# A two-block model on one core: sums over partitions as two float32r products of a high and a low part

## The reference

```python
def rms_norm(x, g):
    y = x32 * lax.rsqrt(jnp.mean(x32 * x32, axis=-1, keepdims=True) + NORM_EPS)
    return y * g

# first block, each of 2 layers: h = rms_norm(x, norm_g); proj = h @ w_in; three branches; x + merged @ w_out
q = apply_rope(rms_norm(qc.reshape(b, t, 4, 128), q_norm), cos_a, sin_a)
k = apply_rope(rms_norm(kc.reshape(b, t, 4, 128), k_norm), cos_a, sin_a)
# beside it the delta-rule branch: a triangular solve of 64x64 blocks, and a top-k of 128 keys
# second block: rmsnorm over 1024, 8 query heads and 2 x 2 key heads of 64, each rmsnormed;
# then h + merged @ w_o, rmsnorm over 1024, h + square(relu(hn @ w_ff1)) @ w_ff2
```

## Time and profile before

| | |
|---|---|
| median of 3 runs | 1946.79 us (1946.22 to 1951.45) |
| profiled execution | 1947.63 us, of which the span of instructions is 1945.8 |
| PE busy | 1931.6 us, 99% of the span |
| PEld busy | 1532.9 us |
| DVE, ACT, POOL busy | 1021.6, 888.9, 851.3 us |
| granted TensorE clock | full in all 40 slices |

### The profile page before, as it was taken

The page is one execution under the profiler, slowest core; times in us unless marked ns, Lnnn a source line. Parts: engine busy times, 40 slices in busy tenths (PEclk is TensorE's granted clock), DMA queues, the critical chain, the costliest instruction groups (busy, mean ns, idle before and its releaser), DMA issues.

```text
span 1945.8 us, 23734 instructions
## 1 busy us (share of the span) xinstructions
PE 1931.6 (99%) x9108; PEld 1532.9 (79%) x9108; DVE 1021.6 (53%) x1832; ACT 888.9 (46%) x1355; POOL 851.3 (44%) x644
## 2 busy tenths in 40 slices
PE   9999999999999999999999999999999999999999
PEld 6878877877788878787877788677766788888887
DVE  5657755555745668666464747574644436101210
ACT  6455553344345455543344355586555444312321
POOL 4545432443445454422434445455322445444443
PEclk9999999999999999999999999999999999999999
DMA  5334542423535235632424545322111332222232
GB/s 202 128 110 135 139 137 73 162 76 118 187 107 175 90 114 147 162 109 71 153 65 141 189 154 162 136 76 98 65 56 55 119 107 89 98 97 98 98 114 71
DMA packets 94864, 227.69 MB, mean 117 GB/s; under 512 B 29880, under 2 KB 32952, under 8 KB 93440
## 3 DMA queue, kind: packets, MB, share of 16 engines
q1 hardware_dynamic: 89056, 223.03, 35.4%
q10 hardware_dynamic: 5696, 3.15, 0.6%
HBM read 194.01 MB, written 24.64 MB: 112 GB/s over the span
## 4 chain that ended last, share of the span: by engine, by line
PE 85%; DVE 7%; DMA 2%; ACT 2%; POOL 1%; SPq 1%; issue 1%; ACTq 0%; DVEq 0%
PE bank L442 84%; DVE ER L376 1%; DVE kv L376 1%; PE bank L446 1%; SPq L371 1%; POOL wl L376 1%; DMA X<-inverses 1%; DMA gt<-gates 1%; DVE scs L401 1%; DMA kv<-blocks 1%; DVE m8s L398 0%; ACT lt L428 0%; DVE lt L386 0%; DVE tmp L376 0%; ACT wh L431 0%
## 5 line engine op out<-in xcount | busy, mean ns | idle before, releaser
L376 POOL TENSOR_TENSOR wl<-st,wh 128x512 fp32r<-128x512 f32 x602 | 804.5, 1359 | 1019.3 <-ACT wh L431 1019.2
L442 PE MATMUL bank<-hh,wh 128*128 128x512 f32 x1616 | 651.8, 404 | 2.8 <-DVE hl L386 0.9
L442 PE MATMUL bank<-hh,wl 128*128 128x512 f32 x1616 | 629.8, 390 | 0.0
L442 PE MATMUL bank<-hl,wh 128*128 128x512 f32 x1616 | 629.3, 390 | 0.0
L431 ACT ACTIVATE wh<-st 128x1024 fp32r<-128x1024 f32 (+1 forms) x302 | 317.0, 1050 | 242.9 <-PE bank L442 194.5
L442 PEld LDWEIGHTS bank<-hh,wh 128*128 128x128 f32 x1616 | 303.4, 188 | 92.5 <-issue 24.6
L442 PEld LDWEIGHTS bank<-hl,wh 128*128 128x128 f32 x1616 | 303.6, 188 | 66.9 <-issue 6.9
L442 PEld LDWEIGHTS bank<-hh,wl 128*128 128x128 f32 x1616 | 303.3, 188 | 64.3
L376 DVE TENSOR_TENSOR xt<-xt,bank 128x512 f32<-128x512 f32 x40 | 27.5, 687 | 235.6 <-PE bank L442 235.6
L428 ACT ACTIVATE tmp<-bank 128x512 f32<-128x512 f32 x70 | 41.7, 596 | 156.8 <-PE bank L442 150.2
L442 PE MATMUL bank<-fh,wh 128*128 128x512 f32 x256 | 99.6, 389 | 0.0
(11 more groups left out here) (344 smaller groups left out, 2838.6 us busy)
## 6 DMA issues: line engine op xcount, KB each, us to landing
st<-units SPq DMA_DIRECT2D x300, 512.0 KB, 3.5
gates<-tmp SPq DMA_DIRECT2D x48, 256.0 KB, 2.8
gt<-gates SPq DMA_DIRECT2D x48, 256.0 KB, 3.7
pads<-tmp SPq DMA_DIRECT2D x32, 128.0 KB, 2.7
qk<-tmp SPq DMA_DIRECT2D x16, 256.0 KB, 4.3
x_scratch<-xt SPq DMA_DIRECT2D x2, 2048.0 KB, 8.7
xt<-x_scratch SPq DMA_DIRECT2D x2, 2048.0 KB, 8.3
ph<-phi SPq DMA_DIRECT2D x8, 512.0 KB, 4.6
```

The costliest lines, as they stand in the source:

```text
L376: return NOTHING if self.e is None else self.e.tensor_tensor(out, a, b, op)
L442: return NOTHING if self.e is None else self.e.matmul(out, lhsT, rhs, start=start, stop=stop, skip_group_check=share)
```

## The change

The constants `onesr`, `meanr` and `blkr` become float32r tiles of their own, filled by DVE at the start out of a zeroed tile, and leave the DMA of constants (961 instead of 1345 columns); older float32 uses read them as float32. For 25 of the 26 sums of 512 columns the squares are given as two float32r parts: a high one, which ACT writes by a second Square (or by a copy of `nacc`), and a low one, which DVE gets by subtracting; PE's `summed` adds two float32r products with the same constant. `norm("in")` keeps its float32 product. In `proj(l)` all follow-up steps from the product on stand one `yield`, half a tile, later; the high and low parts have one buffer each (`sqh`, `sql`), so ACT waits for the product of row c-1 before it writes row c. In `proj2` the last query's and the last key's products stand behind the first of three units of token values.

```diff
+        def summed(out, exact, high, low):
+
+            pe.mm(out, exact, high, True, False)
+            return pe.mm(out, exact, low, False, True)
...
         def norm(w, frees):
             def total():
...
+                if w == "in":
+                    pe.wait_ge(*at("nacc", w, 7))
+                    pe.mm(bank(7, "norm", w), ones, nacc[:], True, True).then_inc(*sig("norm_mm", w))
+                else:
+                    pe.wait_ge(*at("sum_lo", w))
+                    summed(bank(7, "norm", w), onesr[:], tmpr[0][:], tmpr[1][:]).then_inc(*sig("norm_mm", w))
...
             def row(c):
                 yield
-                pe.wait_ge(*at("qk_sq", l, c))
-                pe.mm(bank(3, "qk_mean", l, c), mean, row_tiles(c)[2][:], True, True).then_inc(*sig("qk_mean", l, c))
+                yield
+                pe.wait_ge(*at("qk_lo", l, c))
+                summed(bank(3, "qk_mean", l, c), meanr[:], layer[l].sqh[:], layer[l].sql[:]).then_inc(*sig("qk_mean", l, c))
...
-                pe.wait_ge(*at("q2_sq", c))
-                pe.mm(bank(4, "q2_mm", c), blk, tmp[c % 2][:], True, True).then_inc(*sig("q2_mm", c))
+                yield
+                pe.wait_ge(*at("q2_lo", c))
+                summed(bank(4, "q2_mm", c), blkr[:], oh[:, c, :], ol[:, c, :]).then_inc(*sig("q2_mm", c))
...
+                for j in range(3):
+                    yield tokens(j), idle(1)
```

ACT, in `norm`, `row(c)` and `headnorm`:

```diff
+            if w != "in":
+                ac.wait_ge(*at("nacc", w, 7))
+                ac.cp(tmpr[0][:], nacc[:]).then_inc(*sig("sum_hi", w))
...
                 ac.act(x2[:], x[:], ACT.Square).then_inc(*sig("qk_sq", l, c))
+                if c > 0:
+                    ac.wait_ge(*at("qk_mean", l, c - 1))
+                ac.act(layer[l].sqh[:], x[:], ACT.Square).then_inc(*sig("qk_hi", l, c))
+                yield
                 yield
...
             ac.act(a[:, 0:width], x, ACT.Square, 0.125).then_inc(*sig(*sq))
+            ac.act(high, x, ACT.Square, 0.125).then_inc(*sig(*hi))
+            yield
```

DVE, in `norm`, `row(c)` and `turned`:

```diff
+            if w != "in":
+                dv.wait_ge(*at("sum_hi", w))
+                dv.tt(tmpr[1][:], nacc[:], tmpr[0][:].bitcast(F32), ALU.subtract).then_inc(*sig("sum_lo", w))
...
                 yield
+                dv.wait_ge(*at("qk_hi", l, c))
+                dv.tt(L.sql[:], x2[:], L.sqh[:].bitcast(F32), ALU.subtract).then_inc(*sig("qk_lo", l, c))
                 dv.wait_ge(*at(f"swap{c % 2}", "qk", l, c, 64))
-                dv.wait_ge(*at("qk_sq", l, c))
                 dv.stt(x[:], x[:], K(f"{w}n{l}"), TA("cosA"), ALU.mult, ALU.mult).then_inc(*sig("qk_n", l, c, 0))
                 dv.stt(xs, xs, K(f"{w}swap{l}"), TA("sinA"), ALU.mult, ALU.mult).then_inc(*sig("qk_n", l, c, 1))
+                yield
                 yield
```

More of the change, by code:

```diff
@@ L530, in build @@
     cst = sb("cst", [128, n_cst])
+    onesr, meanr, blkr = [sb(n, [128, 128], F32R) for n in ("onesr", "meanr", "blkr")]
     identr = sb("identr", [128, 128], F32R)
@@ L534, in build @@
     hh, hl = sb("hh", [128, 8, T], F32R), sb("hl", [128, 8, T], F32R)
+    tms = ExitStack()
+    tmpr = [sb(f"tmpr{i}", [128, T], F32R, stack=tms) for i in range(2)]
+    tms.close()
     tmp = [sb(f"tmp{i}", [128, T]) for i in range(4)]
@@ L594, in build @@
         L.cdiag = sb(f"cdiag{l}", [128, 128], stack=dtmp)
+        L.sqh, L.sql = [sb(f"{n}{l}", [128, T], F32R, stack=dtmp) for n in ("sqh", "sql")]
         dtmp.close()
@@ L700, in K @@
         return col[rows, names[name][0] + i:names[name][0] + i + 1]
-    ident, ones, mean, blk, eps = C("ident"), C("ones"), C("mean"), C("blk"), C("eps")
+    ident, eps = C("ident"), C("eps")
+    ones, blk = onesr[:].bitcast(F32), blkr[:].bitcast(F32)
     first = C("first")
@@ L1110, in query, with tokens @@
                 yield
-                pe.wait_ge(*at("q2_sq", c))
-                pe.mm(bank(4, "q2_mm", c), blk, tmp[c % 2][:], True, True).then_inc(*sig("q2_mm", c))
+                yield
+                pe.wait_ge(*at("q2_lo", c))
+                summed(bank(4, "q2_mm", c), blkr[:], oh[:, c, :], ol[:, c, :]).then_inc(*sig("q2_mm", c))
             def key(j):
                 yield
[L1116 to L1127, removed]
+                yield
+                pe.wait_ge(*at("k2_lo", j))
+                summed(bank(5, "k2_mm", j), blkr[:], oh[:, 4 + j, :], ol[:, 4 + j, :]).then_inc(*sig("k2_mm", j))
+            def tokens(j):
                 n = take("v2", j)
@@ L1140, in proj2, with jobs @@
                 t.then_inc(*sig("unit", n))
-                yield
+            def jobs():
+                for j in range(4):
+                    yield (tile(("c2", (512, 640, 768, 1024)[j]), 6 + j % 2, (("kv", "k2")[j // 2], j % 2), "nA"),
+                           both(query(j), idle(1) if j < 2 else key(j - 2)))
+                for j in range(3):
+                    yield tokens(j), idle(1)
+            yield from lagged(jobs())
         def compress():
@@ L1740, in key @@
                 ac.wait_ge(*at(f"free{6 + j}", "k2", j))
[L1741 removed]
+                yield from headnorm(x, tmp[2 + j], T, ("k2_sq", j), ("k2_mm", j), 5, ("k2_r", j), oh[:, 4 + j, :], ("k2_hi", j))
             def jobs():
@@ L2434, in proj2, with turned @@
                 dv.tt(lt[c][:], banks[c][:], nr[:], ALU.mult).then_inc(*sig(f"free{c}", "q2", c))
-            def turned(out, x, w, ws, cos, sin, a, name, swapped, squared, root, last):
+            def turned(out, x, w, ws, cos, sin, a, name, swapped, squared, root, last, low, high, lo):
+                dv.wait_ge(*squared)
+                dv.tt(low, a, high.bitcast(F32), ALU.subtract).then_inc(*sig(*lo))
                 dv.wait_ge(*swapped)
-                dv.wait_ge(*squared)
                 dv.stt(x, x, w, cos, ALU.mult, ALU.mult).then_inc(*sig(*name, 0))
                 dv.stt(out, out, ws, sin, ALU.mult, ALU.mult).then_inc(*sig(*name, 1))
+                yield
                 yield
@@ L2660, in vector_program @@
         dv.set(pad[1][:], 0.0).then_inc(*sig("warm"))
+        zero = pad[1]
+        dv.wait_ge(*at("warm"))
+        dv.ts(onesr[:], zero[:, 0:128], 1.0, ALU.add)
+        dv.ts(meanr[:], zero[:, 0:128], 1.0 / 128.0, ALU.add)
+        for g, r in enumerate(G2):
+            for f, c in enumerate(G2):
+                t = dv.ts(blkr[r, c], zero[r, c], float(f == g), ALU.add)
+        t.then_inc(*sig("exact"))
         dv.wait_ge(*at("col"))
```

26 lines of the change are left out of this document (13 added, 13 removed).

## The result

The changed kernel takes 1995.63 us in the median (1993.03 to 1997.17, 4 runs) against 1947.05 (1946.22 to 1951.45, 4 runs) for the kernel before: ratio 1.0239, 95% interval 1.0226 to 1.0252. The direction is as forecast. The size is not: +48.6 us where +34 was forecast, 2.6 us above the upper end of the range. The profiled execution took 1995.65 us with a span of 1993.8, 48.0 above the span before.

What follows compares the result with a forecast made beforehand. PE bounds the kernel, busy 1931.6 of 1945.8 us. Terms: +30.6 us for both layers' q and k rows, -1.3 norms, +4.7 proj2, together +34.0, so 1981 us; range 1966 to 1993.

Steps and rivals of the forecast that it cites:

- What a product costs: On PE: a float32 product costs 0.88 us, two float32r products 0.45; 25 exchanges save 10.5 us if nobody waits.
- The wait in rows 2 and 3: First block, each layer: PE waits for DVE's low part, 5.0 us at row 2 and 12 at row 3.
- The step that failed: Row 2, DVE: inverse's blocks land 0.84 us earlier with PE, so DVE is ready at 186.16, low part done at 186.85.
- POOL's pause: DVE's inverse between rows 2 and 3: POOL, without weights to split while PE stands, lets DVE finish 4.4 us sooner.
- proj2: Three PE waits of 2.4 us for DVE's subtractions, less six savings of 0.42 us: +4.7 us, bounds -2.5 and +7.
- Norms and all that is left: Three norms: low part ready at about 585.5, before PE asks at 586.72, so hidden; saves 1.3 us.
- The cold start: PE after standing at row 3 runs slow at first: 1.7 us lost once per layer, 0 as the bound.
- more than the wait: Rival: weight splits queue behind ACT's root, so PE's next unit could be late; or no POOL relief; 1993 to 2005, chance 0.09.
- Nobody waits: Rival: DVE's row 3 subtraction is done before PE wants it, about 200 us in layer 0; 1936 us, chance 0.04.
- The range: 1966 to 1993 us; upper end has DVE ready for row 3 at 221.9 in both layers, 6.3 us later than forecast.

Runs made afterwards that it cites:

- e5: Changed kernel with each row's low part made by POOL behind ACT's high part, instead of by DVE; 1970.49 us, ratio 1.0113.
- e10: Kernel before with norms and all rows as two float32r products, low part by POOL, nothing moved, proj2 as before; 1950.14 us, ratio 1.0009.
- e9: Kernel before with only the float32 products and follow-ups of rows 0 and 1 of each layer half a tile later; 1956.95 us, ratio 1.0040.
- e6: Changed kernel with rows 0 and 1 of each layer put back as in the kernel before; 1986.96 us, ratio 1.0198.
- e3: Kernel before with each row's float32 product and follow-ups half a tile later, no high or low parts; 1966.04 us, ratio 1.0084.
- e12: Kernel before with norms and rows 5 to 7 of each layer changed, rows 0 to 4 and proj2 as before; 1949.16 us, ratio 1.0002.
- e4: Changed kernel, but PE's second product reads the high part again and ACT's root waits for the unread low part; 1995.29 us, ratio 1.0240.
- e7: Changed kernel with DVE's subtraction of each row one step earlier in DVE's order; 1986.01 us, ratio 1.0193.
- e8: Kernel before with norms and rows 4 to 7 of each layer changed, rows 0 to 3 and proj2 as before; 1973.64 us, ratio 1.0126.

## Why the prediction was right in kind and short in size

**What a product costs** held: a pair takes 0.47 us behind the inverse, priced 0.45.

**The wait in rows 2 and 3** held as a mechanism: four waits for `sql`, 36.1 us, forecast 34. e5 and e10 show that it is the place in DVE's queue. That the sum of the waits is so close is partly luck: DVE was ready 7 us later than forecast, but PE had by then lost 3.3 us ahead of row tile 2 and 1.4 to the clock behind it, and so came later too.

**The step that failed** is "DVE comes to its row at 187.00, after five steps of the inverse. Those start when the blocks have landed (182.44), a transfer issued behind PE's progress, so 0.84 earlier now". The transfer does not simply move with PE. The follow-ups of rows 0 and 1 are moved too, and they stand ahead of the blocks on three queues. ACT in the changed kernel, root of row tile 1, which now stands behind the product at 166.63:

```profile
167.36 1.28 ACT L417 ACT_TABLE_LOAD   x1 [2.71 <-PE bank L439]
168.66 0.69 ACT L425 ACTIVATE nr<-bank,cst 128x512 f32<-128x512 f32 x1
169.38 0.63 ACT L425 ACTIVATE nr<-nr 128x512 f32<-128x512 f32 x1
```

DVE behind it, first in the changed kernel, then in the kernel before:

```profile
170.11 0.69 DVE L373 TENSOR_TENSOR tmp<-tmp,nr 128x512 f32<-128x512 f32 x1 [3.02 <-ACT nr L425]
...
172.53 0.68 DVE L373 TENSOR_TENSOR lT<-bank,ER 128x512 f32<-128x512 f32 x1
...
181.52 2.37 DVE L389 MEMSET lT<- 32x512 f32 x4 [3.12 <-DMA blocks<-lT]
```

```profile
166.94 0.69 DVE L376 TENSOR_TENSOR tmp<-tmp,nr 128x512 f32<-128x512 f32 x1
...
169.86 0.68 DVE L376 TENSOR_TENSOR lT<-bank,ER 128x512 f32<-128x512 f32 x1
...
176.80 2.37 DVE L392 MEMSET lT<- 32x512 f32 x4 [0.83 <-DMA blocks<-lT]
```

DVE waits 3.0 us for ACT's root before it makes the last head's `lT`, which is 2.7 us later and done at 173.21. Yet this alone does not set the time of the blocks. ACT's next split of a weight unit, POOL's behind it, and SP's issues in the changed kernel:

```profile
171.91 1.05 ACT L428 ACTIVATE wh<-st 128x1024 fp32r<-128x1024 f32 x1
```

```profile
173.03 2.59 POOL L373 TENSOR_TENSOR wl<-st,wh 128x512 fp32r<-128x512 f32 x2 [9.46 <-ACT wh L428]
```

```profile
175.65 0.35 SPq L368 DMA_DIRECT2D st<-units  x1
...
176.52 2.31 SPq L368 DMA_DIRECT2D blocks<-lT  x4
```

ACT splits the unit only behind the root (171.91, before 166.44), POOL has stood idle 9.5 us for it, SP's weight load is issued 0.03 us after POOL's end, and the blocks stand behind that load in SP's queue: 176.52 for 173.07 before, 3.3 us after `lT` is done. They are back 4.7 us later (181.52 for 176.80), and the inverse starts 4.9 us later than before, 5.7 later than forecast. Layer 1 has the same order (load 767.54, blocks 768.41), and so has e9 (177.32, 178.19); in e6, with rows 0 and 1 untouched, the blocks go out at 173.01 as before.

From the start of the inverse to row 3's subtraction it takes 34.6 us, forecast 33.3: POOL's pause gives back 3.1 us (187.31 to 221.93, against 182.44 to 219.46 and the 0.7 of one more subtraction), not 4.4. 5.7 + 1.3 = 7.0 is the whole difference between 22.35 and 15.3. e6 and e9 show the first part from both sides; the second is read from the traces alone.

Over the block the trace gives +22.2 us in layer 0 (from the first `ER` product after 126 us to the one at 339.9 before and 361.8 after) and +22.8 in layer 1. Together 45.0 for a forecast 30.6. `proj2`: +4.6 for a forecast +4.7, from the middle of its first tile (1182.61 before, 1226.31 after) to the last product of token values (1214.79, 1263.07). The size is luck: the three waits are 2.6, 1.6 and 1.2 us, 5.5 in all instead of 3 x 2.4, and a cold start behind the last two (granted clock 0.63 in 1254 to 1258 us, 1.7 us lost) came in addition. Norms and all that is left: 48.0 - 45.0 - 4.6 = -1.6, forecast -1.3.

**The cold start** was there after all four waits, and not of one size. In layer 0, behind 192.60 and 222.66, the next seven or eight starts are some 0.43 us apart (the first 0.59), 1.4 and 1.7 us lost; in layer 1, behind 784.00 and 814.24, it is thirteen and fourteen starts, 2.6 and 2.8 us lost. As the prediction said, the one behind row 2 is swallowed by row 3's wait; the other cost 1.7 and 2.8 where 1.7 was taken for each layer. The granted clock of 0.83 over 182 to 232 us counts the waits too, in whose later part it is down already (0.50 in 216 to 222 us, PE idle). The rule of the Trainium skill, "TensorE: Matmul & The Clock Gate", section "Why this matters for your kernels", that PE drops to 1.2 GHz when it idles long enough between bursts, agrees.

**The rival "more than the wait"** gave the right size (1993 to 2005) for another reason: the trace has no wait for `wl` among PE's first lines. Its mechanism, weight splits queued behind ACT's root, was nevertheless at work: it was looked for on PE, and it fell on SP's queue and so on the blocks. **"Nobody waits"** came nearest in e10, and there the 6.7 us went into waits of 0.5 to 0.7 us. It asked for a low part of row 3 by 200 us; POOL has it at 199.3.

**The range** failed because both its ends varied only what DVE does between row 2 and row 3, and none varied when the inverse starts.

What stays open: the 16.4 us of e3 are 7.8 from rows 0 and 1 (e9). The other 8.6 are read from the two traces and were not run by themselves: against e9, PE in e3 waits 2.5 us more for `nr` at row tile 5, where the chain by way of its buffer ends, has two cold starts more, both behind these waits (3.4), and waits 2.8 us more for `scs` at row tile 6; 8.7 together. Which of the rows 0 and 1 holds the blocks up was not separated either.

## What to carry to other kernels

- A second operand made by a second engine puts the consumer behind that engine's queue. Find the instruction ahead of which the new one stands, take its time from the trace, and then ask what sets that time: here the follow-ups that were moved with the product delayed the start of the very work that it waits for, by way of ACT, POOL and the queue of SP, none of which makes the operand.
- Where an engine is a fixed stretch of work ahead, waits do not add up. Taking away 7 us ahead of row tile 3 brought 5; restricting the change to "safe" rows moved the wait to the next row, because these had been safe only behind the first wait.
- Price a short wait with the clock behind it. Of the 18 us that the later place alone cost in e3, 5 were products at the half rate, in stretches where no wait was longer than 2.3 us.
- An edit that lets one engine pass a wait tells nothing if the next engine must wait for the same thing. Look who waits before reading the time.

## What the runs showed of the hardware

- Short waits did not always leave the clock alone. Around a wait of 1.3 us in e3 (166 to 172 us) and one of 1.9 us in e12 (255 to 264 us) the granted clock is 1.00. But the same wait of e12 in layer 1 (1.97 us, followed by the same products) has the clock at 0.50 in 832 to 834 us; the wait of 2.3 us at row tile 5 of e3 was followed by half-rate products in both layers; and behind a wait of 1.35 us in e9, followed by four products of 32 rows and four of 64 rows, the 512-column products start 0.43 us apart, with a granted clock of 0.73 in 144 to 150 us. The first of the two waits of e3, in layer 0:

```profile
241.66 1.25 PE L448 MATMUL bank<-nr,meanr 128*128 128x512 f32 x2 [2.29 <-ACT nr L434]
...
243.55 0.63 PE L448 MATMUL bank<-hh,wl 128*128 128x512 f32 x1
```

- Each wait of 6 us and more in the changed kernel, e4, e5, e7 and e8 had a cold start. It has no fixed price: behind row tile 3 of the changed kernel it cost 1.7 us in layer 0 and 2.8 in layer 1.
- DVE is quicker beside an idle POOL, but only a little: of 14 and 18 us of POOL's pause 3.1 us of DVE's inverse came back. With POOL busier (e5) DVE took 37.6 us from row 2's to row 3's multiplications instead of 32.5 before, and its multiplication of row 3 took 1.77 us instead of 0.74.
